# First weight piece and x in four pairs of 256 rows, first two tiles accumulated together, second piece's low part on VectorE

## The chip, the cores and the metric

The kernel runs on one core of one Trainium2 chip. The metric is the time of one execution on the device in microseconds (us); the time before is the median of 3 runs.

## The reference

Two layers of a streaming encoder trunk on x of 512 tokens by 1024 channels, float32. Each layer is

```
x <- LN(alpha * x + Mix(x))
x <- LN(alpha * x + MoE(x))
```

Mix multiplies x by one input projection (`h = x @ w_in + b_in`, 1024 to 1792 columns) and gives the columns to three groups: a gated causal depthwise convolution of 31 taps (256 channels, `a * sigmoid(g)`), a sliding-window attention of 8 query and 2 key heads with rotation of the first 16 dimensions, and a gated spatial mixing. Their 1024 outputs go through `w_out`. MoE is a router that picks 2 of 16 experts for each token, and a SwiGLU with 512 hidden channels in each expert.

## The kernel before

**Precision.** Each float32 matrix product is made from three products of a faster type: both operands are split into a high part (ScalarE's copy, which rounds) and a low part (the rest, by a subtraction on VectorE or GpSimd), and TensorE adds high x high, low x high and high x low (`product`, L392). So an operand takes three steps before TensorE can use it: transfer, high, low.

**Pieces.** The columns of `w_in` are reordered (gate half of the convolution first, then its value half, then q, k and v, the rest) and loaded in seven pieces of 256 columns and all 1024 rows (1 MB each, `load_piece`, L291); three further-on pieces come from `w_out`. Raw pieces go to two buffers `wraw` in turn, split pieces to three slots `wh`/`wl` in turn. In the traces `wraw` has the name `w_gate`, because it lies in that buffer, and x before its split has the name `w_up`. ScalarE makes a piece's high part (`piece`, L785), with `piece_high` counting them. GpSimd makes the low parts of pieces 1 to 8 of layer 0 (`piece_lows`, L1440), and VectorE that of piece 0 (L1324); `piece_low` counts them. SyncE issues all loads in order; piece q waits for `piece_low` >= q - 1.

**Tiles.** A piece gives two tiles of 128 output channels by 512 tokens (`channels(q, m)`, L403): 8 row blocks of 128 times three products, 24 in all, into one PSUM bank. Layer 0 begins with `channels(0, 0)`, `channels(1, 0)`, `channels(0, 1)`, `channels(1, 1)` (L434 to L437) into banks 0 to 3, each counted in `proj_done`. Later tiles go to banks 0 and 1 in turn and wait until the tile two before was read (`proj_act`, `proj_dve`). The sixth tile, `channels(2, 1)`, so waits for `gate_conv(1)`, which reads bank 3.

**The start.** SyncE issues piece 0, x in four parts of 256 rows (512 KB each), a table, piece 1 and further tables. ScalarE copies piece 0, then the four x parts, then piece 1. VectorE makes piece 0's low part and then the four of x, and TensorE's first tile waits for the x parts one by one.

**VectorE's queue in the projection of layer 0** is in a fixed order (L1329 on): `gate_conv(0)` (L1041; it waits for `proj_done` 2 and ScalarE's sigmoid, and is the first user of the tiles), the 31 taps of the first 128 channels (L1053 to L1057), `gate_conv(1)` before its seventeenth tap, then the taps of the other 128 channels with five rotations (`rope`, L1028) strewn in: L1032 multiplies the permuted tile (PSUM) by the sine, L1033 the tile by the cosine (both in SBUF), L1034 adds (both in SBUF). Then `mask_set`, for which the first scores on TensorE wait.

**ScalarE's queue** has the tiles' copies out of PSUM (L810, L818 and following) with the high parts of later pieces among them at fixed places: piece 5 behind the sixth tile's copy, piece 6 behind the eighth's, piece 7 behind the tenth's. GpSimd makes each low part when its high part is there.

## Time and profile before

| | us |
|---|---|
| median of the runs | 1137.98 (1137.33 to 1139.25) |
| profiled execution | 1142.18 |
| its span | 1140.4 |
| TensorE busy | 965.8 (85%) |
| VectorE busy | 807.7 (71%) |
| ScalarE busy | 648.9 (57%) |
| GpSimd busy | 521.6 (46%) |

The span is what the profile shows from the first to the last instruction; the execution's own time is 1.8 us more. The engines are named PE (TensorE's products), DVE (VectorE), ACT (ScalarE), POOL (GpSimd) and SP (SyncE, which issues the loads); a "q" behind a name is the engine's sequencer. L12 is line 12 of the kernel. A clock of 1.00 is TensorE's full clock, 2.4 GHz. Shares of the whole span mix stages with different limits, so the stages have to be read one by one.

### The profile page before, as it was taken

The numbers are of one execution on the slowest core, as the hardware profiler recorded it, in microseconds if no ns is written. First come the engines' busy times: TensorE is split into PE (matmuls) and PEld (weight loads), VectorE is DVE, ScalarE is ACT, GpSimd is POOL, SyncE is SP. The second block draws the span as 40 slices with busy tenths as digits, with TensorE's granted clock in tenths as the row PEclk, the third lists the DMA queues.
The fourth block names the chain that finished last, engine by engine and source line by source line (L and its number), as shares of the span: only waits on it lengthen the run. The fifth ranks groups of instructions, "written<-read, shape, count | busy, mean of one in ns | idle before, by whom it ended". The sixth has DMA issues, their size and how long they took to land. (4 is left out here: it accounts for less than half of the span.)

```text
span 1140.4 us, 15102 instructions
## 1 busy us (share of the span) xinstructions
PE 965.8 (85%) x4700; PEld 780.4 (68%) x4700; DVE 807.7 (71%) x964; ACT 648.9 (57%) x723; POOL 521.6 (46%) x297
## 2 busy tenths in 40 slices
PE   4998998289999999999269979982899999999950
PEld 3866775168888887878268757751688888888840
DVE  2996755567778787777467967555677787878737
ACT  4224712078878887877213347120788787878730
POOL 3435354035656556565205453440356565564621
PEclk9998998679999999999679989986799999999985
DMA  8521183079999999963713211930799999999625
GB/s 271 187 81 39 57 331 147 1 263 360 373 368 366 381 355 371 364 264 108 227 38 111 74 46 51 336 146 3 265 373 378 370 357 372 352 370 367 255 114 143
DMA packets 122511, 268.99 MB, mean 236 GB/s; under 512 B 10608, under 2 KB 26128, under 8 KB 121968
## 3 DMA queue, kind: packets, MB, share of 16 engines
q1 hardware_dynamic: 110192, 243.99, 59.0%
q0 software_dynamic: 12288, 24.60, 6.7%
q8 instruction: 17, 0.28, 0.1%
q14 instruction: 14, 0.11, 0.0%
HBM read 263.38 MB, written 24.64 MB: 253 GB/s over the span
## 5 line engine op out<-in xcount | busy, mean ns | idle before, releaser
L1500 POOL TENSOR_TENSOR wl<-w_down,wh 128x2048 fp32r<-128x2048 f32 x33 | 151.6, 4595 | 165.5 <-ACT wh L937 165.5
L1026 DVE TENSOR_TENSOR wl<-w_gate,wh 128x2048 fp32r<-128x2048 f32 x71 | 166.0, 2339 | 58.3 <-ACT wh L937 30.4
L1026 DVE TENSOR_TENSOR wl<-w_up,wh 128x2048 fp32r<-128x2048 f32 x66 | 151.2, 2293 | 29.5 <-ACT wh L937 29.1
L702 PE MATMUL bank<-wh,xTh 128*128 128x512 f32 x528 | 143.4, 394 | 4.5 <-ACT wh L937 4.5
L937 ACT ACTIVATE wh<-w_down 128x2048 fp32r<-128x2048 f32 x66 | 126.8, 1921 | 30.0 <-PE bank L702 30.0
L702 PE MATMUL bank<-wh,xTl 128*128 128x512 f32 x528 | 142.8, 393 | 0.0
L702 PE MATMUL bank<-wl,xTh 128*128 128x512 f32 x528 | 142.8, 393 | 0.0
L937 ACT ACTIVATE wh<-w_up 128x2048 fp32r<-128x2048 f32 x66 | 126.5, 1917 | 25.5 <-PE bank L720 24.9
L1444 POOL TENSOR_TENSOR wl<-w_gate,wh 128x2048 fp32r<-128x2048 f32 x17 | 78.0, 4593 | 135.5 <-ACT wh L794 135.2
L1026 DVE TENSOR_TENSOR xTl<-bank,xTh 128x512 fp32r<-128x512 f32 (+1 forms) x168 | 89.9, 574 | 62.5 <-ACT xTh L941 24.7
L396 PE MATMUL bank<-xTh,wh 128*128 128x512 f32 (+2 forms) x272 | 112.2, 412 | 24.9 <-DVE xTl L1026 21.1
L937 ACT ACTIVATE wh<-w_gate 128x2048 fp32r<-128x2048 f32 x66 | 126.5, 1916 | 7.7 <-PE bank L720 7.7
L702 PEld LDWEIGHTS bank<-wh,xTh 128*128 128x128 f32 x528 | 100.3, 190 | 26.2 <-issue 5.3
L702 PEld LDWEIGHTS bank<-wh,xTl 128*128 128x128 f32 x528 | 100.3, 190 | 21.1
L702 PEld LDWEIGHTS bank<-wl,xTh 128*128 128x128 f32 x528 | 100.3, 190 | 21.0
L396 PE MATMUL bank<-xTh,wl 128*128 128x512 f32 (+2 forms) x272 | 105.4, 387 | 0.0
L396 PE MATMUL bank<-xTl,wh 128*128 128x512 f32 (+2 forms) x272 | 105.1, 386 | 0.0
L1479 POOL DMA_INDIRECT moemem<-x_rows,gather_idx x35 | 81.6, 2330 | 30.6 <-POOL gather_idx L1476 30.6
L941 ACT ACTIVATE xTh<-bank 128x512 fp32r<-128x512 f32 x66 | 39.1, 593 | 92.4 <-PE bank L674 92.4
L396 PEld LDWEIGHTS bank<-xTh,wh 128*128 128x128 f32 (+1 forms) x272 | 53.8, 198 | 41.3 <-issue 17.9
L1026 DVE TENSOR_TENSOR wl<-w_down,wh 128x2048 fp32r<-128x2048 f32 x33 | 75.7, 2293 | 7.9 <-ACT wh L937 7.9
L1057 DVE SCALAR_TENSOR_TENSOR bank<-w_down,col,bank 128x512 f32<-128x512 f32 x116 | 77.7, 747 | 1.7 <-DVE w_down L1041 0.5
(206 smaller groups left out, 1726.5 us busy)
## 6 DMA issues: line engine op xcount, KB each, us to landing
w_up<-in_exp_w_up SPq DMA_DIRECT2D x32, 2048.0 KB, 13.3
w_down<-in_exp_w_down SPq DMA_DIRECT2D x32, 2048.0 KB
w_gate<-in_exp_w_gate SPq DMA_DIRECT2D x32, 2048.0 KB, 12.6
w_gate<-in_w_in SPq DMA_DIRECT2D x14, 1024.0 KB, 5.5
w_gate<-in_w_out SPq DMA_DIRECT2D x8, 1024.0 KB, 5.0
x_rows<-xtok POOLq DMA_DIRECT2D x8, 512.0 KB, 3.0
w_gate<-in_rows_mix SPq DMA_DIRECT2D x2, 1536.0 KB, 6.3
w_up<-in_x_t SPq DMA_DIRECT2D x4, 512.0 KB, 7.5
```

Of the source, the lines that this page charges most:

```text
L396: mm = pe.matmul(out, xs[i], ws[k], start=(first and n == 0), stop=(last and n == 2))
L702: mm = pe.matmul(bank[piece][:, :], xgT[m][:, 4 * (i % 2) + k, :], w[q][:, k, :], start=(i % 2 == 0 and n == 0 and k == 0), stop=(i % 2 == ...
L937: act.activation(wh[s][:, :], slot[r][p][:, cols], ACT.Copy).then_inc(half_high, 1)
L941: act.activation(xgT[0][:, 4 * i:4 * i + 4, :], bank[2 + i][:, :].rearrange("p (k t) -> p k t", k=4), ACT.Copy).then_inc(xgT_high, 1)
L1026: return dve.tensor_tensor(out, src, high.bitcast(F32), ALU.subtract)
L1057: y = dve.scalar_tensor_tensor(o, x, wk, o, ALU.mult, ALU.add)
L1444: pool.tensor_tensor(wl[n % SLOTS][:, :], wraw[n % 2], wh[n % SLOTS][:, :].bitcast(F32), ALU.subtract)\
L1479: pool.indirect_dma_start(xg, None, x1d[l], bass.IndirectOffsetOnAxis(ap=gather_idx[:, :], axis=0), bounds_check=T - 1, oob_is_err=False). ...
L1500: pool.tensor_tensor(wl[s][:, :], slot[r][p][:, cols], wh[s][:, :].bitcast(F32), ALU.subtract)\
```

## The change

Layer 0 only. SyncE loads the first piece in four parts of 256 rows, each followed by the x part of the same rows (`head`), and ScalarE and VectorE split them in this order. TensorE runs along the four pairs and accumulates both tiles of the first piece, in banks 0 and 2, 12 products for each pair; then come the two tiles of the second piece, in banks 1 and 3. `proj_done` then counts bank 0, bank 2, bank 1, bank 3, so `gate_conv(0)` waits for a count of 3. VectorE, not GpSimd, makes the second piece's low part. GpSimd begins with piece 2.

```diff
--- before.py
+++ after.py
@@ -197,6 +197,8 @@
         wexp_in = [[sem(f"{n}_in{r}") for n in ("gate", "up", "down")] for r in range(2)]
         dve_chain, pool_chain = sem("dve_chain"), sem("pool_chain")
         xT_high, xT_low = sem("xT_high"), sem("xT_low")
+        head_in = [sem(f"head_in{i}") for i in range(4)]
+        head_high, head_low = sem("head_high"), sem("head_low")
         piece_high, piece_low, last_low = sem("piece_high"), sem("piece_low"), sem("last_low")
         proj_done = sem("proj_done")
         proj_act, proj_dve = sem("proj_act"), sem("proj_dve")
@@ -261,6 +263,10 @@
 
             return bank[4 + 2 * (j % 2) + i] if q % 2 else bank[4 * i + j]
 
+        def head(x, i):
+
+            return x[:, 512 * i:512 * i + 512].rearrange("p (k n) -> p k n", k=2)
+
         def halves(i):
 
             return i // 2, slice(2048 * (i % 2), 2048 * (i % 2) + 2048), i % SLOTS
@@ -318,12 +324,13 @@
 
             for l in range(DEPTH):
                 if l == 0:
-                    load_piece(l, 0)
-                    sp.dma_start(xraw[:, 0:2, :], a["x_t"][0:256, :].rearrange("(k p) t -> p k t", p=P))\
-                      .then_inc(xT_in[0], 16)
-                    for i in range(1, 4):
-                        sp.dma_start(xraw[:, 2 * i:2 * i + 2, :], a["x_t"][256 * i:256 * i + 256, :]
-                                     .rearrange("(k p) t -> p k t", p=P)).then_inc(xT_in[i], 16)
+                    for i in range(4):
+                        rows = slice(256 * i, 256 * i + 256)
+                        sp.dma_start(head(wraw[0], i), a["w_in"][l, rows, 0:PIECE].rearrange("(k p) n -> p k n", p=P))\
+                          .then_inc(head_in[i], 16)
+                        sp.dma_start(xraw[:, 2 * i:2 * i + 2, :], a["x_t"][rows, :].rearrange("(k p) t -> p k t", p=P))\
+                          .then_inc(xT_in[i], 16)
+                    sp.sem_inc(wraw_in[0], 16)
                     sp.dma_start(col[:, :], a["cols"][l]).then_inc(col_in, 16)
                     load_piece(l, 1)
                     sp.dma_start(cst[:, :], a["const"]).then_inc(const_in, 16)
@@ -413,8 +420,6 @@
                     n = (PIECES * l + q) % SLOTS
                     w = [x[:, :].rearrange("p (k n) -> p k n", k=KD) for x in (wh[n], wl[n])]
                     for k in range(KD):
-                        if l == 0 and t == 0 and k % 2 == 0:
-                            pe.wait_ge(xT_low, k // 2 + 1)
                         mm = product(bank[t if t < 4 else t % 2][:, c], [w[i][:, k, P * m:P * m + P] for i in range(2)],
                                      [xparts[i][:, k, c] for i in range(2)], k == 0, k == KD - 1)
                     if part != 0:
@@ -431,10 +436,19 @@
                     pe.matmul(bank[4 + n % 2][:, :], perm, src, start=True, stop=True).then_inc(rot_done, 1)
 
                 if l == 0:
-                    channels(0, 0)
-                    channels(1, 0)
-                    channels(0, 1)
-                    channels(1, 1)
+                    w = [x[:, :].rearrange("p (k n) -> p k n", k=KD) for x in (wh[0], wl[0])]
+                    for i in range(4):
+                        pe.wait_ge(head_low, i + 1)
+                        pe.wait_ge(xT_low, i + 1)
+                        for m in range(2):
+                            for k in (2 * i, 2 * i + 1):
+                                mm = product(bank[2 * m][:, :], [w[h][:, k, P * m:P * m + P] for h in range(2)],
+                                             [xparts[h][:, k, :] for h in range(2)], k == 0, k == KD - 1)
+                            if i == 3:
+                                mm.then_inc(proj_done, 1)
+                    for t in (1, 3):
+                        task[0] = t
+                        channels(1, t // 2)
                 else:
                     q = 2 * l - 1
                     turn(q, 0)
@@ -795,11 +809,14 @@
 
             def project(l):
                 if l == 0:
-                    piece(l, 0)
                     for i in range(4):
+                        act.wait_ge(head_in[i], 16)
+                        act.activation(head(wh[0], i), head(wraw[0], i), ACT.Copy).then_inc(head_high, 1)
                         act.wait_ge(xT_in[i], 16)
                         act.activation(xparts[0][:, 2 * i:2 * i + 2, :], xraw[:, 2 * i:2 * i + 2, :], ACT.Copy)\
                            .then_inc(xT_high, 1)
+                    act.wait_ge(head_high, 4)
+                    act.sem_inc(piece_high, 1)
                     piece(l, 1)
                 act.wait_ge(col_in, 16 * (l + 1))
                 for m in range(2):
@@ -1036,7 +1053,7 @@
 
             def gate_conv(l, m):
 
-                dve.wait_ge(proj_done, PROJ * l + 2 * m + 2)
+                dve.wait_ge(proj_done, PROJ * l + (3 if l == 0 and m == 0 else 2 * m + 2))
                 dve.wait_ge(sig_set, 2 * l + m + 1)
                 link(dve.scalar_tensor_tensor(glu[:, m, TAPS - 1:], bank[2 * m + 1][:, :],
                                               col[:, C_BIN + 2 + m:C_BIN + 3 + m], u[:, m, :], ALU.add, ALU.mult))
@@ -1320,12 +1337,15 @@
             dve.sem_inc(he_set, 1)
             link(dve.memset(eps, EPS))
             link(dve.memset(mhalf, -0.5))
-            dve.wait_ge(piece_high, 1)
-            low(wl[0][:, :], wraw[0], wh[0][:, :]).then_inc(piece_low, 1)
             for i in range(4):
+                dve.wait_ge(head_high, i + 1)
+                low(head(wl[0], i), head(wraw[0], i), head(wh[0], i)).then_inc(head_low, 1)
                 dve.wait_ge(xT_high, i + 1)
                 low(xparts[1][:, 2 * i:2 * i + 2, :], xraw[:, 2 * i:2 * i + 2, :], xparts[0][:, 2 * i:2 * i + 2, :])\
                     .then_inc(xT_low, 1)
+            dve.wait_ge(head_low, 4)
+            dve.sem_inc(piece_low, 1)
+            piece_lows(0, 1)
             for l in range(DEPTH):
                 dve.wait_ge(col_in, 16 * (l + 1))
                 link(dve.memset(glu[:, :, 0:TAPS - 1], 0.0))
@@ -1512,8 +1532,8 @@
             for l in range(DEPTH):
                 if l == 0:
 
-                    pool.wait_ge(piece_low, 1)
-                for q in range(1 if l == 0 else 3, 7):
+                    pool.wait_ge(piece_low, 2)
+                for q in range(2 if l == 0 else 3, 7):
                     piece_lows(l, q)
 
                 piece_lows(l, 7)
```

## Rows read from the trace of the kernel before

**Rows 1.** Stretches: from:to and length, busy us of each engine, PE clock, DMA share, GB/s.
```profile
39.90:52.00 12.10, 12.10 (x53) 9.70 (x52) 11.72 (x20) 3.89 (x4) 6.60 (x2) 1.00 0.56 175
52.00:90.00 38.00, 33.84 (x163) 26.43 (x161) 36.36 (x51) 10.76 (x12) 13.79 (x3) 0.96 0.24 83
232.00:580.00 348.00, 314.67 (x1447) 256.68 (x1446) 263.06 (x216) 257.72 (x231) 182.69 (x109) 0.95 0.87 314
```

**Rows 2.** Waits of TensorE, 0 to 140 us: who for whom, total, times, longest.
```profile
PE bank L396 <- DVE xTl L1026: 11.9, 1, 11.9
PE bank L536 <- DVEq L1347: 2.8, 1, 2.8
PE bank L396 <- POOL wl L1444: 2.5, 1, 2.5
```

**Rows 3.** Waits of all engines, 80 to 110 us.
```profile
POOL w_down L1522 <- DVEq L1353: 6.8, 1, 6.8
```

**Rows 4.** Instructions in time order, 0 to 22 us: start, duration, engine, line, operation.
```profile
6.28 1.91 ACT L794 ACTIVATE wh<-w_gate 128x2048 fp32r<-128x2048 f32 x1 [4.18 <-DMA w_gate<-in_w_in]
...
8.30 2.29 DVE L1026 TENSOR_TENSOR wl<-w_gate,wh 128x2048 fp32r<-128x2048 f32 x1 [6.98 <-ACT wh L794]
...
10.51 4.62 DVE L1026 TENSOR_TENSOR xTl<-w_up,xTh 128x1024 fp32r<-128x1024 f32 x4
...
11.75 1.06 ACT L801 ACTIVATE xTh<-w_up 128x1024 fp32r<-128x1024 f32 x1 [0.33 <-DMA w_up<-in_x_t]
...
11.88 0.77 PE L396 MATMUL bank<-xTh,wh 128*128 128x512 f32 x1 [11.88 <-DVE xTl L1026]
...
14.88 1.92 ACT L794 ACTIVATE wh<-w_gate 128x2048 fp32r<-128x2048 f32 x1 [2.08 <-DMA w_gate<-in_w_in]
...
18.71 0.39 PE L396 MATMUL bank<-xTl,wh 128*128 128x512 f32 x1
19.19 1.28 ACT L810 ACT_TABLE_LOAD   x1 [2.39 <-PE bank L396]
...
21.91 1.91 ACT L794 ACTIVATE wh<-w_gate 128x2048 fp32r<-128x2048 f32 x1 [0.74 <-DMA w_gate<-in_w_in]
```

**Rows 5.** Stretches of one us each: DMA share and GB/s come last.
```profile
2.00:3.00 1.00, 0.00 (x0) 0.00 (x0) 0.00 (x0) 0.11 (x1) 0.00 (x0) 1.00 0.74 175
3.00:4.00 1.00, 0.00 (x0) 0.00 (x0) 0.00 (x0) 0.00 (x0) 0.00 (x0) 1.00 1.02 358
4.00:5.00 1.00, 0.00 (x0) 0.00 (x0) 0.00 (x0) 0.00 (x0) 0.00 (x0) 1.00 1.08 379
```

**Rows 6.** VectorE in time order, 29 to 70 us.
```profile
29.01 0.75 DVE L1041 SCALAR_TENSOR_TENSOR w_down<-bank,col,w_down 128x512 f32<-128x512 f32 x1 [13.80 <-PE bank L396]
...
40.59 0.74 DVE L1041 SCALAR_TENSOR_TENSOR w_down<-bank,col,w_down 128x512 f32<-128x512 f32 x1
...
55.83 2.60 DVE L1033 TENSOR_TENSOR w_gate<-w_gate,w_down 128x512 f32<-128x512 f32 x1
...
63.39 0.69 DVE L1034 TENSOR_TENSOR w_gate<-w_gate,w_down 128x512 f32<-128x512 f32 x1
...
68.90 2.22 DVE L1033 TENSOR_TENSOR w_gate<-w_gate,w_down 128x512 f32<-128x512 f32 x1
```

**Rows 7.** ScalarE and GpSimd in time order, 50 to 70 us.
```profile
50.72 0.69 ACT L818 ACTIVATE w_gate<-bank,col 128x512 f32<-128x512 f32 x1 [4.75 <-PE bank L396]
...
53.28 4.60 POOL L1444 TENSOR_TENSOR wl<-w_gate,wh 128x2048 fp32r<-128x2048 f32 x1 [6.77 <-ACT wh L794]
65.98 4.59 POOL L1444 TENSOR_TENSOR wl<-w_gate,wh 128x2048 fp32r<-128x2048 f32 x1 [8.09 <-ACT wh L794]
```

**Rows 8.** TensorE behind a wait: two stretches with clock, and the second wait.
```profile
19.50:24.50 5.00, 2.94 (x8) 2.31 (x9) 0.00 (x0) 3.57 (x3) 2.61 (x2) 0.74 0.69 198
152.00:155.00 3.00, 2.71 (x12) 2.21 (x13) 0.24 (x1) 0.00 (x0) 3.00 (x2) 1.00 1.05 414
...
152.29 0.50 PE L396 MATMUL bank<-wh,xTh 128*128 128x512 f32 x1 [1.42 <-DVE xTl L1026]
```

## The prediction

> **What bounds the kernel now.** I read four views in this order: the busy times of stretches, the waits, the first 22 us in order of time, and then VectorE's and GpSimd's own timelines up to 90 us.
>
> The stretches [rows 1] show two kinds of stage. In the expert stage TensorE is busy 315 of 348 us: nothing of the change is there. In the projection of layer 0 TensorE and VectorE are both full: from 39.9 to 52 us VectorE is busy 11.72 of 12.10 us, from 52 to 90 us 36.36 of 38. Which of the two sets the end is told by the waits [rows 2]: TensorE waits 11.9 us for the first split of x, 2.5 us for the second weight piece (GpSimd's low part), and then 2.8 us at the first scores, for a VectorE semaphore (mask_set). GpSimd also waits 6.8 us for VectorE there [rows 3]. VectorE has no such wait for TensorE after its first real work at 29.01 us [rows 6]. So until the scores the chain is: start of VectorE's gate_conv(0) at 29.01, then its queue of taps and rotations without a gap. TensorE is ahead of it and loses its lead by waiting at the end. Whatever moves VectorE's start, or shortens its queue, moves the rest.
>
> **Step 1, the first product.** Now TensorE starts at 11.88 [rows 4], behind a 1 MB piece copied whole (1.91 us), its low (2.29) and the first x low. With the change it needs 256 KB of weights and 512 KB of x. Bytes delivered by the end of each us [rows 5]: 0.19 MB at 3, 0.55 at 4, 0.93 at 5 (with 0.01 before 2). The old first piece, 1.05 MB, is reached at 5.33, and its copy starts at 6.28: 0.95 us later. The new first pair is 0.79 MB, reached at 4.63; I take 1.0 us for the landing: ScalarE's copy of x starts at 5.63 (its copy of the 256 KB is done by then: 4.2 to 4.8, a quarter of 1.91 plus overhead), takes 1.06 (the row of the x part), 0.11 passes to VectorE (6.28 + 1.91 to 8.30), and from the start of an x low to the first product is 1.37 (10.51 to 11.88). First product T = 5.63 + 1.06 + 0.11 + 1.37 = 8.2, so 3.7 earlier. Bounds: 7.2 if the landing costs nothing, 11.88 if the pair arrives no sooner than piece and x do now.
>
> **Step 2, the start of VectorE's queue.** gate_conv(0) reads bank 1, which is now the third tile, not the second. A tile is 24 products. The first tile's 24 starts spread over 6.83 us (11.88 to 18.71), because the clock rises only on the way; afterwards a product takes 0.228 us (53 products in 12.10 us, [rows 1]). The reader of a tile starts 0.48 after its last product starts (18.71 to 19.19). So gate_conv(0) starts at S = T + 6.83 + 48 x 0.228 + 0.48 = T + 18.3 = 26.4, if TensorE never stops on the way. Against 29.01 that is **2.6 us earlier**. The extra tile in front (5.5 us) eats more than the earlier start alone gives; the rest comes from two removed losses: the 2.5 us wait for piece 1, and the slow clock behind it [rows 8].
>
> Does TensorE stop? Pairs: 768 KB come every 2 us at 380 GB/s, ScalarE needs about 0.6 + 1.06 for a pair, VectorE 0.6 + 1.16 (4.62 over four, [rows 4]), TensorE 12 x 0.228 = 2.7 or more: TensorE is the slowest, and no pair is late. The last pair's x copy starts as now at 11.75, since the bytes ahead of it are the same, and VectorE ends its low near 14.1, while TensorE needs it at T + 36 products, near 18. Piece 1: same bytes ahead, so its copy starts at 14.88 as now and ends at 16.8; VectorE's low (2.29, where GpSimd takes 4.6, [rows 7]) ends at 19.2. TensorE asks for it at T + 6.83 + 25 x 0.228 = 20.7. Cover: 1.4 us; each us beyond that costs a us. The low delays nothing on VectorE, which is idle until 26.4.
>
> SyncE issues three more transfers (about 0.5 us each) ahead of piece 1, but all are issued by about 6 us, long before their bytes flow. Piece 2's issue waits for piece_low 1, which moves from 10.6 (8.30 + 2.29) to 14.1. Its copy starts at 21.91 now [rows 4], 7.8 us after that, and 1 MB at 380 GB/s is 2.8 us: nothing. ScalarE makes this copy behind the sigmoid of bank 0; bank 0 ends at T + 6.83 + 18 x 0.228 + 0.48, about 19.6 against 19.19, so this slips by at most 0.4; its low is ready near 29 (1.9 + 4.6 behind), and TensorE asks for it one tile behind S, near 31.6. Piece 3's copy waits for proj_done 3 as before, the end of the third tile, which comes earlier now.
>
> **Step 3, the stalls inside VectorE's queue.** Rope multiplies x by cosine, both in SBUF (L1033). This takes 0.69 us, but 2.60 at 55.83 and 2.22 at 68.90 [rows 6], and both times GpSimd's piece low runs (53.28 to 57.88, 65.98 to 70.57, [rows 7]); the multiply ends 0.55 us behind it. Taps and the PSUM sources keep their length beside GpSimd. So an SBUF-only operation of VectorE stands still until GpSimd's is over.
>
> The Trainium skill ("SBUF — State Buffer", section "SBUF: two separate sides") says that the pair of ports shared by both is an exclusive lock for the whole instruction, also for a VectorE operation with two SBUF inputs. By that rule, the trace agrees (2.60 against 0.69), and the sum is the same by row and by rule.
>
> What matters is where the lows fall after the change. TensorE's fifth tile ends near T + 6.83 + 96 x 0.228 + 0.3, about 37.1, and the sixth must wait until gate_conv(1) has read bank 3: now that ends 11.58 + 0.74 behind the queue's start (29.01 to 40.59, [rows 6]), so it starts at S + 12.4 = 38.8. TensorE idles 1.7 us, and from here both engines are locked relative to S. The sixth tile is copied 5.7 later, S + 18.1, and the piece low starts 2.56 behind this copy (50.72 to 53.28, [rows 7]): S + 20.7 to S + 25.3. The first L1033 is at S + 26.8: free, 1.91 us saved. The next low is 12.70 later, S + 33.4 to 38.0; the third rope's L1033 comes at 39.9 - 1.9 = S + 38.0: just free, 1.53 saved. The low after that (12.7 later again, S + 46.1 to 50.7) meets the fifth rope's multiply at about S + 50.4 (a rope every 6.2 us: the second's last operation at 63.39, so its multiply at 62.7, and the third's at 68.90); I count nothing. Sum of step 3: **3.4 us**. Bounds: 0 (all stay) and below nothing, see the rivals.
>
> **Carry.** At the scores TensorE, ScalarE and GpSimd wait for VectorE [rows 2, 3], all orders behind are relative to that, and the expert stage takes its time from TensorE. So 2.6 + 3.4 = 6.0 us reach the end. The profiled execution took 1142.18 (span 1140.4 and 1.8 around it), which gives 1136.2; the median of the runs is 4.2 lower, 1137.98, and gives **1132.0**.
>
> **Rivals.**
> (a) The clock falls in the new 1.7 us wait before tile six. For: behind the 2.5 us wait the granted clock is 0.74 of full over 5 us [rows 8]. Against: a wait of 1.42 at 152.29 left it at 1.00 (2.4 GHz). Price: TensorE 1.4 later (6.83 against 24 x 0.228), so the second low covers the third rope again: 1.4 of the 3.4 is lost, time 1133.4.
> (b) Only the head start comes, the collisions stay in number because the lags behind a tile differ from those I carried over: 2.6 gained, 1135.4. For: the second rests on a margin near 0.
> (c) The pairs don't land one by one but close together. For: eight transfers are outstanding at once. Against: rows 5 with the copies at 6.28, 11.75 and 14.88 show landing in order of issue. With T = 11.88 again, S = 30.1, 1.1 later than now, and step 3, which hangs on S alone, still gives 3.4: 1135.7. The Trainium skill ("DMA: Bandwidth & Descriptors", section "Anatomy of one DMA — SWDGE (gpsimd) path") gives a fixed part of about 2.0 us for each transfer, measured on another issue path than this one; if it were paid one after another, four x parts could not have been copied by 12.8 us as they are, so the trace speaks against that reading.
> (d) Slower: GpSimd's lows land on the rope before. The second rope's two SBUF operations end near S + 33.2 (63.39 + 0.69 - 29.01 - 1.91, [rows 6]), and the low begins at S + 33.4. If it began before S + 32.5, that is 0.9 sooner relative to VectorE than I find, it would hold the second operation until 37.1 + 0.55: 4.4 us. The fourth rope's multiply, due at S + 44.2 and now at 48.6, would then meet the next low until 50.7 + 0.55, 2.6 more. 7.0 lost against 6.0 gained: 1139.0. Up to that point it costs nothing; from there it decides.
>
> **Chances.** Forecast 0.52, (a) 0.13, (b) 0.18, (c) 0.10, (d) 0.07. Under 0.2% (2.3 us) from 1137.98 a measurement here can't tell a change; that is 1135.7. Faster: forecast, (a), most of (b), half of (c), together 0.80. Same: the rest of (b) and (c), 0.13. Slower: 0.07. The range reaches down to 1129.8 (T at 7.2, another us in the ropes behind) and up to 1136.5, which holds (b) and (c) and leaves out (d).
>
> **What would show it.** First product near 8.2, no wait of TensorE between pairs or at the third tile, L1041 first at 26.4; the first and third L1033 at 0.69; a wait of TensorE of about 1.7 before tile six, its clock at full behind it; scores 6 us earlier, and the same 6 us at the first expert. Wrong would be: a first product after 10, a wait for piece 1, any L1033 or L1034 over 2 us, or a gain at the scores that is gone at the experts.

## The result, and the profile after

| | median | runs | |
|---|---|---|---|
| before, same chip | 1138.62 us | 1137.33 to 1140.45 | 4 |
| changed | 1146.88 us | 1143.21 to 1148.92 | 4 |

The ratio is 1.0068, 95% interval 1.0038 to 1.0097: the change made the kernel 0.7% slower, where 1132.0 us was forecast. Repeated on another chip it gave 1144.59 against 1138.36, ratio 1.0059 (1.0032 to 1.0085). The profiled execution took 1143.21 us, the lowest of its runs, while that of before, 1142.18, was above all the runs shown with it. The two traces alone thus differ by 1 us, the medians by 6 to 8; where it can be done I compare several executions.

First the head of the kernel. This is the timeline of the changed kernel up to 39 us (start, duration, engine, line, operation; in brackets the idle time before and what ended it), against [rows 4]:
```profile
3.81 0.63 ACT L814 ACTIVATE wh<-w_gate 128x512 fp32r<-128x512 f32 x1 [1.71 <-DMA w_gate<-in_w_in]
...
5.17 1.06 ACT L816 ACTIVATE xTh<-w_up 128x1024 fp32r<-128x1024 f32 x1 [0.73 <-DMA w_up<-in_x_t]
...
6.26 1.23 DVE L1043 TENSOR_TENSOR xTl<-w_up,xTh 128x1024 fp32r<-128x1024 f32 x1 [1.02 <-ACT xTh L816]
...
7.63 0.77 PE L403 MATMUL bank<-xTh,wh 128*128 128x512 f32 x1 [7.63 <-DVE xTl L1043]
...
12.98 1.06 ACT L816 ACTIVATE xTh<-w_up 128x1024 fp32r<-128x1024 f32 x1 [0.53 <-DMA w_up<-in_x_t]
...
16.12 1.92 ACT L808 ACTIVATE wh<-w_gate 128x2048 fp32r<-128x2048 f32 x1 [2.08 <-DMA w_gate<-in_w_in]
...
18.07 2.29 DVE L1043 TENSOR_TENSOR wl<-w_gate,wh 128x2048 fp32r<-128x2048 f32 x1 [2.77 <-ACT wh L808]
...
26.27 0.75 DVE L1058 SCALAR_TENSOR_TENSOR w_down<-bank,col,w_down 128x512 f32<-128x512 f32 x1 [5.84 <-PE bank L403]
...
38.71 0.50 PE L403 MATMUL bank<-xTh,wh 128*128 128x512 f32 x1 [1.66 <-DVEq L1060]
```
The first product comes at 7.63 (was 11.88), VectorE's queue starts at 26.27 (was 29.01), and TensorE's wait ahead of the sixth tile is 1.66: 8.2, 26.4 and 1.7 had been forecast. That part did what it should.

The waits of TensorE from 0 to 140 us (who for whom, total, times, longest) answer to [rows 2]:
```profile
PE bank L550 <- DVEq L1367: 9.0, 1, 9.0
...
PE bank L403 <- DVE xTl L1043: 7.6, 1, 7.6
...
PE bank L436 <- DVEq L1052: 2.0, 1, 2.0
...
PE bank L403 <- DVEq L1060: 1.7, 1, 1.7
```
The wait for piece 1 (2.5) is gone and the one for x is 4.3 shorter, but the wait at the scores is 9.0 instead of 2.8, and ahead of it, at 65.83, there is a new one of 2.0 for L1052, the end of the second rope. The scores start at 88.21, against 85.66 before: of 2.7 us of head start nothing is left, and 2.6 are lost. The stretches show the same as [rows 1] do, TensorE's busy time in the second of them falling from 33.84 to 26.86 us while VectorE stays full:
```profile
39.90:52.00 12.10, 12.10 (x52) 9.26 (x51) 11.97 (x16) 3.78 (x4) 7.32 (x2) 1.00 0.62 211
52.00:90.00 38.00, 26.86 (x125) 20.74 (x124) 36.50 (x48) 7.64 (x7) 9.19 (x2) 0.90 0.24 83
```

Where VectorE loses it is on its own timeline (compare [rows 6]) beside GpSimd's (compare [rows 7]). A low of GpSimd is here the subtraction that makes the low part of one piece:
```profile
48.95 2.80 DVE L1358 CAST utri<-w_down 128x128 bf16<-128x128 f32 x1
...
55.66 0.69 DVE L1050 TENSOR_TENSOR w_gate<-w_gate,w_down 128x512 f32<-128x512 f32 x1
...
60.59 4.32 DVE L1050 TENSOR_TENSOR w_gate<-w_gate,w_down 128x512 f32<-128x512 f32 x1
...
76.69 3.46 DVE L1050 TENSOR_TENSOR w_gate<-w_gate,w_down 128x512 f32<-128x512 f32 x1
```
```profile
47.07 4.59 POOL L1464 TENSOR_TENSOR wl<-w_gate,wh 128x2048 fp32r<-128x2048 f32 x1 [4.43 <-ACT wh L808]
...
59.76 4.59 POOL L1464 TENSOR_TENSOR wl<-w_gate,wh 128x2048 fp32r<-128x2048 f32 x1 [8.11 <-ACT wh L808]
...
75.01 4.59 POOL L1464 TENSOR_TENSOR wl<-w_gate,wh 128x2048 fp32r<-128x2048 f32 x1 [10.65 <-ACT wh L808]
```
L1050 is the multiply of a rope (L1033 before); shown are the first, second and fourth, and the third and fifth took 0.69. The first one is now free, as forecast. But a cast of a 128 x 128 constant in front of it took 2.80 us: GpSimd's low ran from 47.07 to 51.66, and the cast ended 0.09 us behind it. Before, the cast took 0.23 us. Two rows of before that the prediction did not use, the cast and the fifth rope:
```profile
51.69 0.23 DVE L1338 CAST utri<-w_down 128x128 bf16<-128x128 f32 x1
...
82.91 0.92 DVE L1033 TENSOR_TENSOR w_gate<-w_gate,w_down 128x512 f32<-128x512 f32 x1
```
VectorE is 2.57 us late from there. The second low of GpSimd starts at 59.76, the second rope's multiply comes at 60.59 and ends only at 64.91 (4.32 us). TensorE waits 2.0 us for the end of this rope, and the third low comes 15.25 us behind the second, where the prediction had 12.7. It begins at 75.01, the fourth rope's multiply at 76.69: 3.46. Excess over the undisturbed lengths: 2.57 + 3.63 + 2.77 = 8.97 us. Before it was 1.91 + 1.53 + 0.23 = 3.67 for the first, third and fifth rope. The difference, 5.3 us, is the whole of what lies between VectorE's start and the scores (88.21 - 26.27 = 61.94, before 85.66 - 29.01 = 56.65).

### The profile page after: what moved, and what is told of

It reads as the page before. It is cut to its first block and busy times, and to the rows that moved or that the text cites. A ratio compares the mean times of both kernels' runs of the same rounds, so it can differ in the third digit from the quotient of the medians.

```text
span 1141.4 us, 15117 instructions
## 1 busy us (share of the span) xinstructions
PE 965.4 (85%) x4700; PEld 778.2 (68%) x4700; DVE 814.7 (71%) x968; ACT 650.0 (57%) x726; POOL 520.0 (46%) x296
## 5 line engine op out<-in xcount | busy, mean ns | idle before, releaser
L1043 DVE TENSOR_TENSOR wl<-w_gate,wh 128x2048 fp32r<-128x2048 f32 (+1 forms) x75 | 168.8, 2252 | 55.7 <-ACT wh L954 27.6
L1464 POOL TENSOR_TENSOR wl<-w_gate,wh 128x2048 fp32r<-128x2048 f32 x16 | 73.5, 4603 | 136.1 <-ACT wh L808 135.7
```

The lines of the kernel that those rows point to most:

```text
L1043: return dve.tensor_tensor(out, src, high.bitcast(F32), ALU.subtract)
L1464: pool.tensor_tensor(wl[n % SLOTS][:, :], wraw[n % 2], wh[n % SLOTS][:, :].bitcast(F32), ALU.subtract)\
```

## The experiments

Milestones of all the profiled executions, in us: S, the start of VectorE's queue (its first read of bank 1); the scores; TensorE's 1.42 us wait late in layer 0's mixing; the first tile of layer 1; the same 1.42 us wait in layer 1; the first expert of layer 1; TensorE's last product.

| kernel | S | S to scores | scores | late mixing | layer 1 | late mixing 1 | expert, layer 1 | expert to end |
|---|---|---|---|---|---|---|---|---|
| before | 29.01 | 56.65 | 85.66 | 152.29 | 579.66 | 723.14 | 801.26 | 297.2 |
| before_again | 27.21 | 56.65 | 83.86 | 150.26 | 576.55 | 717.41 | 795.40 | 297.2 |
| before_pad7 | 27.43 | 56.64 | 84.07 | 148.88 | 574.74 | 718.47 | 796.82 | 298.7 |
| changed | 26.27 | 61.94 | 88.21 | 152.74 | 578.46 | 722.15 | 800.36 | 299.1 |
| after_again | 26.92 | 61.95 | 88.87 | 153.62 | 579.76 | 723.38 | 801.31 | 299.0 |
| pool_low1 | 29.51 | 63.52 | 93.03 | 159.44 | 586.13 | 729.88 | 807.97 | 297.5 |
| pairs_old_order | 26.84 | 56.63 | 83.47 | 149.89 | 577.29 | 720.62 | 798.79 | 298.9 |
| cast_early | 26.83 | 53.18 | 80.01 | 144.84 | 571.35 | 715.01 | 793.12 | 299.0 |
| cast_taps | 26.83 | 53.50 | 80.33 | 145.75 | 572.10 | 715.82 | 794.09 | 298.8 |
| cast_pool | 26.30 | 53.15 | 79.45 | 145.69 | 571.99 | 715.79 | 794.30 | 297.1 |
| dve_low1 | 25.27 | 56.65 | 81.92 | 147.30 | 573.80 | 717.53 | 795.95 | 297.4 |
| dve_low1_taps | 25.68 | 56.69 | 82.37 | 145.55 | 571.43 | 722.71 | 800.50 | 297.4 |
| dve_low1_taps0 | 24.86 | 56.79 | 81.65 | 143.25 | 568.81 | 712.79 | 790.74 | 297.1 |

And the times. The kernels from one entry in the column of before to the next ran on one chip and share its runs of the kernel before; the ratio is to those, with its 95% interval.

| kernel | median us | runs | before, same chip | ratio |
|---|---|---|---|---|
| after_again | 1144.59 | 5 | 1138.36 | 1.0059 (1.0032 to 1.0085) |
| cast_early | 1135.43 | 10 | | 0.9971 (0.9962 to 0.9981) |
| pool_low1 | 1148.44 | 4 | | 1.0081 (1.0056 to 1.0107) |
| cast_taps | 1135.28 | 8 | | 0.9968 (0.9954 to 0.9983) |
| dve_low1 | 1135.95 | 10 | 1137.68 | 0.9976 (0.9960 to 0.9991) |
| pairs_old_order | 1140.58 | 9 | | 1.0036 (1.0023 to 1.0049) |
| dve_low1_taps | 1139.68 | 10 | | 1.0020 (1.0003 to 1.0036) |
| before_again | 1136.38 | 1 | | |
| cast_pool | 1134.27 | 8 | 1138.29 | 0.9967 (0.9951 to 0.9983) |
| before_pad7 | 1140.13 | 12 | | 1.0014 (1.0003 to 1.0025) |
| dve_low1_taps0 | 1133.78 | 6 | | 0.9959 (0.9944 to 0.9974) |

**after_again**: the changed kernel, nothing edited.

> The changed kernel, unaltered, for a second profile and a second set of times. Theory A (stalls of VectorE's queue behind GpSimd's lows of pieces 5, 6 and 7: the cast of utri 2.80, the multiply of the second rope 4.32, that of the fourth 3.46): the three stalls are there again at the same offsets from the start of the queue (22.7, 34.3 and 50.4 us behind it), together near 9.0 us, and the first scores start near 88.2 us. Rival B (the time is lost behind the scores, in the attention, the expert stages or layer 1, and the first projection has nothing to do with it): the scores near 88.2 again, but the second profile's span is several us over the first's 1141.4 with the first 88 us alike.

Measured 1144.59 us. The three long operations are there again, and from S to the scores it takes 61.95 us against 61.94: the loss is of the program, not of one execution.

**cast_early**: the changed kernel with the cast moved in front of VectorE's first read of a bank, where VectorE is idle.

```diff
                 link(dve.memset(glu[:, :, 0:TAPS - 1], 0.0))
+                if l == 0:
+                    dve.wait_ge(mixc_in, 16)
+                    dve.tensor_copy(utri[:, :], mixc[:, M_UTRI:M_UTRI + P]).then_inc(ones_set, 1)
                 gate_conv(l, 0)
...
-                if l == 0:
-                    dve.wait_ge(mixc_in, 16)
-                    dve.tensor_copy(utri[:, :], mixc[:, M_UTRI:M_UTRI + P]).then_inc(ones_set, 1)
```

> The changed kernel with the cast of utri put before gate_conv(0), where VectorE is idle. Theory A: the cast takes 0.2 us there; the queue then reaches the ropes 2.8 us earlier, ahead of GpSimd's low of piece 6, so the second rope's multiply takes 0.69; the third's may meet the end of that low (under 1.2), the fourth's is free, the fifth's may meet the low of piece 7. Stalls together 2 us in place of 9.0, first scores near 81 us in place of 88.2, and the time 6 to 8 us under the changed kernel's. Rival B: scores earlier, but the time stays within 2 us of the changed kernel's.

Measured 1135.43 us, 9.2 below the changed kernel in the same runs, from the place of one instruction of 0.23 us. VectorE's timeline, the cast and the multiplies of the second and fourth rope (the third took 0.81, the fifth 0.94):
```profile
21.08 0.23 DVE L1354 CAST utri<-w_down 128x128 bf16<-128x128 f32 x1
...
58.43 0.69 DVE L1050 TENSOR_TENSOR w_gate<-w_gate,w_down 128x512 f32<-128x512 f32 x1
...
71.02 0.69 DVE L1050 TENSOR_TENSOR w_gate<-w_gate,w_down 128x512 f32<-128x512 f32 x1
```
and GpSimd's, the two lows that had caught the ropes:
```profile
60.33 4.59 POOL L1464 TENSOR_TENSOR wl<-w_gate,wh 128x2048 fp32r<-128x2048 f32 x1 [8.09 <-ACT wh L808]
...
73.02 4.62 POOL L1464 TENSOR_TENSOR wl<-w_gate,wh 128x2048 fp32r<-128x2048 f32 x1 [8.10 <-ACT wh L808]
```
With the cast gone the second rope starts 1.90 ahead of the low at 60.33, and the fourth 2.00 ahead of the next. The scores start at 80.01, S + 53.18, where after_again has S + 61.95: 8.8 sooner. The rule of the stalls and the prediction's arithmetic of them (3.4 us off the 56.65 of before) are confirmed: the scores come 3.47 sooner behind S, 3.30 from shorter multiplies and the rest from the cast's own place in the queue. What the prediction lacked was the cast.

**cast_taps**: cast_early, and one or two taps moved between the ropes, so that no rope touches a low.

```diff
-                for n, hi in enumerate((8, 14, 20, 26)):
+                for n, hi in enumerate((8, 15, 21, 27)):
...
-                    taps(1, hi - (4 if n == 0 else 6), hi)
+                    taps(1, (4, 8, 15, 21)[n], hi)
...
-                taps(1, 26, TAPS)
+                taps(1, 27, TAPS)
```

> cast_early, and one tap more between the second and the third rope (taps 8 to 15, 15 to 21, 21 to 27 in place of 8 to 14, 14 to 20, 20 to 26), so that the third and fifth ropes' multiplies come 0.7 us later, behind GpSimd's lows of pieces 6 and 7. Theory A: no operation of VectorE in the projection is stretched by over 0.3 us, first scores near 79.5 us, time 1 to 2 us under cast_early's. Rival B: the time is cast_early's.

Measured 1135.28 us, the same as cast_early (1135.43), where 1 to 2 less were expected. All five multiplies are at 0.69, but the extra tap stands ahead of the scores (S + 53.50 against 53.18). A rest of stall of 0.37 us was not worth the 0.7 us of one more tap ahead of the scores.

**pool_low1**: the changed kernel with the second piece's low back on GpSimd.

```diff
-            piece_lows(0, 1)
             for l in range(DEPTH):
                 dve.wait_ge(col_in, 16 * (l + 1))
...
-                    pool.wait_ge(piece_low, 2)
-                for q in range(2 if l == 0 else 3, 7):
+                    pool.wait_ge(piece_low, 1)
+                for q in range(1 if l == 0 else 3, 7):
```

> The changed kernel with the low part of piece 1 made by GpSimd, as before the change; pairs and order of tiles stay. GpSimd takes 4.6 us in place of 2.3, so the third tile starts near 22.7 in place of 20.3 and the clock may fall in that wait of about 2: VectorE's queue starts at 28.5 to 30 in place of 26.3. Theory A: everything behind hangs on that start, so the same three stalls follow at the same offsets, scores near 90.5 to 92, time 2 to 4 us over the changed kernel. Rival B: no change or any.

Measured 1148.44 us, 3.9 over the changed kernel on the same chip. TensorE waits 2.99 us for the piece, and S is 29.51:
```profile
23.67 0.50 PE L403 MATMUL bank<-xTh,wh 128*128 128x512 f32 x1 [2.99 <-POOL wl L1463]
```
The same three operations stand still, the last one for longer:
```profile
52.18 2.79 DVE L1357 CAST utri<-w_down 128x128 bf16<-128x128 f32 x1
...
63.81 4.31 DVE L1050 TENSOR_TENSOR w_gate<-w_gate,w_down 128x512 f32<-128x512 f32 x1
...
79.90 5.07 DVE L1050 TENSOR_TENSOR w_gate<-w_gate,w_down 128x512 f32<-128x512 f32 x1
```
So the low on VectorE is what gives the head start (2.6 of it), and the stalls don't come from it: they come with the order of tiles.

**dve_low1**: the kernel before, and only the second piece's low moved to VectorE.

```diff
+            piece_lows(0, 1)
             for l in range(DEPTH):
                 dve.wait_ge(col_in, 16 * (l + 1))
...
-                    pool.wait_ge(piece_low, 1)
-                for q in range(1 if l == 0 else 3, 7):
+                    pool.wait_ge(piece_low, 2)
+                for q in range(2 if l == 0 else 3, 7):
```

> The kernel before with one part of the change alone: the low part of piece 1 by VectorE (2.3 us) in place of GpSimd (4.6). Theory A: the second tile starts at 19.2 in place of 21.56, without a wait, so the clock stays up and VectorE's queue starts near 25.2, earlier than with the whole change (26.3). TensorE then doesn't wait before its sixth tile, so GpSimd's lows of pieces 5, 6 and 7 stand later against the queue: the cast stays at 0.23, the first rope's multiply meets a low (about 3.2), the third's too (about 2.2), the fifth's perhaps. First scores near 82.5, time 3 to 4 us under the kernel before. Rival C (the earlier start of the queue is what does the harm, however it comes): the cast or the second rope's multiply over 2 us, and no gain.

Measured 1135.95 us, ratio 0.9976. VectorE's queue starts at 25.27, sooner than in any kernel of the change, and both stalls of before stay:
```profile
25.27 0.75 DVE L1041 SCALAR_TENSOR_TENSOR w_down<-bank,col,w_down 128x512 f32<-128x512 f32 x1 [6.21 <-PE bank L396]
...
52.09 2.60 DVE L1033 TENSOR_TENSOR w_gate<-w_gate,w_down 128x512 f32<-128x512 f32 x1
...
65.16 2.23 DVE L1033 TENSOR_TENSOR w_gate<-w_gate,w_down 128x512 f32<-128x512 f32 x1
```
The whole gain of the start is in this one edit; the four pairs and the order of tiles bring VectorE nothing over it (26.3 to 26.9). The gain in time is 1.7 us where 3 to 4 were expected: the S of before to compare with is 27.2 or 27.4, as before_again and before_pad7 show, not 29.01.

**pairs_old_order**: the changed kernel, but the pairs feed bank 0 alone, and the tiles then follow as before.

```diff
-                        for m in range(2):
-                            for k in (2 * i, 2 * i + 1):
+                        for k in (2 * i, 2 * i + 1):
...
-                    for t in (1, 3):
-                        task[0] = t
-                        channels(1, t // 2)
+                    task[0] = 1
+                    channels(1, 0)
+                    channels(0, 1)
+                    channels(1, 1)
```

> The changed kernel with the old order of tiles: only the first half of the first piece is multiplied along the pairs, then channels(1,0), (0,1), (1,1). The first tile ends near 17, TensorE waits about 3.5 for piece 1 and its clock falls, VectorE's queue starts near 27.9. Theory A: TensorE does not wait before its sixth tile, so the lows stand as in the kernel before: cast 0.23, first and third rope's multiply stretched to about 2.8 and 2.2, second and fourth 0.69; scores near 84.9, time 0.5 to 1.5 us under the kernel before. Rival C: as the queue starts 1.1 us earlier than before, cast or second rope over 2 us and a loss.

Measured 1140.58 us, slower than before where somewhat faster was expected. TensorE has nothing to do between the first tile and piece 1:
```profile
19.50 0.80 PE L403 MATMUL bank<-xTh,wh 128*128 128x512 f32 x1 [3.39 <-DVE wl L1043]
```
The cast is free again while the multiplies are as long as before:
```profile
49.52 0.23 DVE L1358 CAST utri<-w_down 128x128 bf16<-128x128 f32 x1
...
53.66 2.58 DVE L1050 TENSOR_TENSOR w_gate<-w_gate,w_down 128x512 f32<-128x512 f32 x1
...
66.72 2.21 DVE L1050 TENSOR_TENSOR w_gate<-w_gate,w_down 128x512 f32<-128x512 f32 x1
```
From S to the scores it takes 56.63 us, as in the kernel before. So, with the same queue of VectorE, it is the order of tiles that decides which operations are caught. TensorE has no wait before its sixth tile here, and the first of the three lows starts at S + 24.3, as before; in the changed kernel it is S + 20.8. The scores come at 83.47, 0.4 sooner than in before_again, and yet the kernel's median is 2.9 us higher. The table shows where 1.7 of it is: expert to end 298.9 against 297.2, a loss that is in the changed kernel as well and does not lie in layer 0. The rest, 1.2 us, stays open. This set off the third group of runs.

**dve_low1_taps**: dve_low1, the cast moved as in cast_early, and the taps between the ropes as (7, 11, 17, 23, 29), in both layers.

```diff
-                taps(1, 0, 4)
-                for n, hi in enumerate((8, 14, 20, 26)):
+                taps(1, 0, 7)
+                for n, hi in enumerate((11, 17, 23, 29)):
```

> dve_low1 with the cast where VectorE is idle and three taps more ahead of the first rope (taps 7, 11, 17, 23, 29 in place of 4, 8, 14, 20, 26), which puts every rope between two of GpSimd's lows. Theory A: all five multiplies at 0.7, mask_set at a time near 82 (the ropes end 2 us later in the queue, the stalls of 4 us are gone), scores near 82 but the last tap 3 to 4 us earlier than in dve_low1; time 1 to 3 us under dve_low1's, the lowest of all. Rival B: no better than dve_low1.

Measured 1139.68 us: a miss. Layer 0 gained (late mixing at 145.55 against 147.30 in dve_low1), though its third rope's multiply still took 2.22 us where 0.7 was expected. But the same cuts in layer 1 brought its ropes under GpSimd's lows:
```profile
630.72 5.02 DVE L1033 TENSOR_TENSOR w_gate<-w_gate,w_down 128x512 f32<-128x512 f32 x1
...
647.53 3.48 DVE L1033 TENSOR_TENSOR w_gate<-w_gate,w_down 128x512 f32<-128x512 f32 x1
```
From the first tile of layer 1 to its late mixing it takes 151.3 us against 143.7.

**before_again**: the kernel before, nothing edited, for one more profile.

> The kernel before, unaltered, for a second profile: the first took 4 us more than the median of its timed runs. Theory A: the first 85.66 us are the same (cast 0.23, first and third rope's multiply 2.6 and 2.2), and the 4 us lie elsewhere. Rival D: the first profile had stretched operations in the first projection that a usual execution has not, so the loss of the change at the scores, 2.55 us by the two profiles, is understated.

It took 1136.38 us. The first 86 us are not those of the first trace. The stretch of [rows 8] and the products behind the wait for piece 1:
```profile
19.50:24.50 5.00, 3.16 (x15) 2.58 (x15) 0.00 (x0) 3.89 (x3) 2.61 (x2) 1.00 0.69 215
```
```profile
21.37 0.50 PE L396 MATMUL bank<-xTh,wh 128*128 128x512 f32 x1 [1.84 <-POOL wl L1444]
...
27.21 0.75 DVE L1041 SCALAR_TENSOR_TENSOR w_down<-bank,col,w_down 128x512 f32<-128x512 f32 x1 [12.21 <-PE bank L396]
```
TensorE waited 1.84 us instead of 2.5, and its granted clock stayed at 1.00 (2.4 GHz) where it had been 0.74. S is 27.21, 1.8 sooner, and from S on everything is equal up to the scores (56.65 both times). So 29.01 was the bad side of a chance; before_pad7, for TensorE the same kernel up to here, has 27.43. The three traces differ first within the first tile. Its products start 0.43 us apart and later 0.23; the step comes after 7 intervals in before, 10 in before_again and 13 in before_pad7. The later the first tile ends, the shorter is the wait for piece 1: 2.46, 1.84 and 1.34 us. Behind the wait of 2.46 the products are 0.43 apart again for 8 intervals, behind the other two they are not.

**cast_pool**: cast_early, but the cast on GpSimd, which changes VectorE's program by one instruction.

```diff
-                    dve.wait_ge(mixc_in, 16)
-                    dve.tensor_copy(utri[:, :], mixc[:, M_UTRI:M_UTRI + P]).then_inc(ones_set, 1)
...
+                    pool.wait_ge(mixc_in, 16)
+                    pool.tensor_copy(utri[:, :], mixc[:, M_UTRI:M_UTRI + P]).then_inc(ones_set, 1)
                     pool.wait_ge(piece_low, 2)
```

> The changed kernel with the cast of utri made by GpSimd, before its first low, while both are idle. VectorE has one instruction less than in cast_early. Theory A: ropes as in cast_early (0.69 to 0.94), first scores near 80.0. Theory E (place of the code): in the profiles so far a pair of experts of layer 1 takes 36.43 us in the kernels with 747, 748 and 750 counted VectorE instructions and 36.63 in those with 751, with VectorE 0.6 us longer at the branch back of the loop over pairs; so with 750 the stage of layer 1, first gathered transposition to TensorE's last, is 297.3 in place of 299.0, and the time 1.5 to 2 us under cast_early's 1135.4. Against E: 299.0 again and the time of cast_early.

**before_pad7**: the kernel before with seven small memsets at the beginning of VectorE's program, where it is idle.

```diff
             link(dve.memset(mhalf, -0.5))
+            for _ in range(7):
+                link(dve.memset(idle[:, :], 0.0))
```

> The kernel before with seven tiny memsets more on VectorE while it waits for the first piece; they take well under 1 us of its 7 us of idle time and write an unused cell. Theory E: the code behind them moves by at least as much as in the changed kernel, VectorE's gap at the branch of the pair loop in layer 1 grows by 0.6 us, the expert stage of layer 1 takes 299.0 in place of 297.2, time 1.5 to 2 us over the kernel before. Against E: 297.2 and no change of the time. Either way the profile shows once more where gate_conv(0) starts in the kernel before: 29.0 as in the first profile or 27.2 as in the second.

These two belong together. before_pad7 is slower than before by 1.8 us (1140.13, ratio 1.0014), with 298.7 from the expert to the end; cast_pool has 297.1, as the kernel before, and took 1134.27 us. That its time lies below cast_early's is not shown by the times alone: against the kernel before on their own chips the ratios are 0.9967 and 0.9971, well within each other's intervals. Take VectorE's instructions as the profile's page counts them, each turn of a loop for itself (the numbers in the expectation are lower by 217 throughout): before has 964, the dve_low1 kernels 965, pool_low1 and cast_pool 967, and all of these have 297.1 to 297.5. The changed kernel, after_again, pairs_old_order, cast_early and cast_taps have 968, before_pad7 has 971, and these have 298.7 to 299.1. What is lost is seen in VectorE's waits from 812 to 1080 us, the experts of layer 1 (who for whom, total, times, longest). Before:
```profile
DVE xTl L1026 <- issue: 9.7, 7, 1.4
```
Changed:
```profile
DVE xTl L1043 <- issue: 11.7, 7, 2.0
```
before_pad7:
```profile
DVE xTl L1026 <- issue: 11.6, 7, 2.0
```
cast_pool:
```profile
DVE xTl L1043 <- issue: 9.5, 7, 1.4
```
There is a gap of VectorE in which it waits for nothing that the profile shows once in each turn of the loop over pairs of experts, where the loop branches back. In before all seven are 1.4 us; in the changed kernel the first is 2.0 and the six others 1.6 (together the 11.7 above). The first one in the changed kernel, and TensorE's wait that follows from it:
```profile
836.81 0.41 DVE L1304 TENSOR_TENSOR moemem<-bank,moemem 128x256 f32<-128x256 f32 x1
...
839.18 0.69 DVE L1043 TENSOR_TENSOR xTl<-bank,xTh 128x512 fp32r<-128x512 f32 x1 [1.96 <-issue]
...
840.25 0.96 PE L734 MATMUL bank<-wh,xTl 128*128 128x512 f32 x3 [0.20 <-DVE xTl L1043]
```
From one such gap to the next it takes 36.63 us instead of 36.43. The 0.6 us expected for every gap holds for the first one only; the others grow by 0.24. The loss goes with the number of VectorE instructions, and before_pad7 shows that instructions without any use are enough for it. How instructions ahead of a loop make its branch longer, and whether their place or their number counts, no run shows. Layer 0's loop is not touched: from its first expert to layer 1 it takes 348.3 to 349.5 us in all kernels, on either side of the count.

**dve_low1_taps0**: dve_low1, the cast moved, and the taps between the ropes changed in layer 0 alone.

```diff
-                taps(1, 0, 4)
-                for n, hi in enumerate((8, 14, 20, 26)):
+                cuts = (7, 11, 19, 25, 31) if l == 0 else (4, 8, 14, 20, 26)
+                taps(1, 0, cuts[0])
+                for n, hi in enumerate(cuts[1:]):
```

> dve_low1 with the cast where VectorE is idle and with the ropes of layer 0 alone moved (taps 7, 11, 19, 25, 31; layer 1 as before, where the earlier move of both layers stretched two multiplies to 5.0 and 3.5). Queue start near 25.5. Theory A: no multiply of layer 0 over 1.1 us, first scores near 82.3 (the ropes now end the queue), layer 1 as in dve_low1; time 2 to 3 us under dve_low1's 1136. Rival B: dve_low1's time, since the scores come no earlier.

Measured 1133.78 us (1131.57 to 1134.68), ratio 0.9959 (0.9944 to 0.9974): the lowest median of the study, below both the kernel before and the changed one (1.0059 and 1.0068 of before). Its interval overlaps those of cast_pool, cast_taps and cast_early, so that it is faster than these is not shown. It keeps the kernel before's loads and its order of tiles. The first and third rope in VectorE's timeline:
```profile
24.86 0.75 DVE L1041 SCALAR_TENSOR_TENSOR w_down<-bank,col,w_down 128x512 f32<-128x512 f32 x1 [5.50 <-PE bank L396]
...
53.54 0.81 DVE L1033 TENSOR_TENSOR w_gate<-w_gate,w_down 128x512 f32<-128x512 f32 x1
...
66.13 0.91 DVE L1033 TENSOR_TENSOR w_gate<-w_gate,w_down 128x512 f32<-128x512 f32 x1
```
The scores come no sooner than in dve_low1, since all 31 taps now stand ahead of them, but what had followed the scores is shorter: late mixing at 143.25 against 147.30.

## Why the prediction was wrong, step by step

**Step 1, right.** First product at 7.63, forecast 8.2. VectorE's first low of x started at 6.26, where 6.80 had been worked out (5.63 + 1.06 + 0.11); ScalarE's copy of x started at 5.17, so by the bytes of [rows 5] (0.79 MB at 4.63) the landing costs 0.5 and not the 1.0 us assumed.

**Step 2, right in its place, with two flaws.** S = 26.27 for 26.4, no wait between pairs, none at the third tile, 1.66 before the sixth. But the bytes being the same did not keep the times: the fourth x copy came at 12.98 instead of 11.75, and piece 1's at 16.12 instead of 14.88, with its low ready at 20.36. The second x copy came 3.57 us behind the first, where 2 us for a pair had been reckoned; the other two followed in 2.13 and 2.11. Of the cover of 1.4 us next to nothing was left: in after_again TensorE waited 0.33 for it, in cast_early 0.74. The second flaw is that 29.01 was read as the kernel's start, when it was one execution's: it holds a fall of the clock that [rows 8] showed and I counted as a loss the change removes. In before_again and before_pad7 it did not happen. The head start over such executions is 0.3 to 1.2 us (26.27 and 26.92 against 27.21 and 27.43), not 2.6. An execution profiled 4.2 us above the median of the runs was the hint. The 6.83 us of the first tile are one execution's as well: 7.47 in before_again, 7.97 in before_pad7, 6.90 in the changed kernel. That the clock rises on the way is seen in the distance of the products, 0.43 and then 0.23 us; the profile's granted clock is 1.00 throughout the stretch.

**Step 3, failed, and this decides the sign.** "So an SBUF-only operation of VectorE stands still until GpSimd's is over": true. The low was forecast at S + 20.7 and began at S + 20.8. I then looked at the ropes alone. The cast from L1338 of before (L1358 after) is SBUF-only too and stood in the queue between the taps, at 51.69 = S + 22.7, in the middle of the forecast low. It was in the trace at 0.23 us and looked free, because before the change no low ran beside it: the next began 1.4 us behind its end. The low was moved off the first rope onto the cast; VectorE then came 2.57 late to the second low, whose margin for the second rope had been worked out as 0.9. From there rival (d) took its course, at its places (second and fourth rope) and almost at its price (the second rope's multiply 3.63, the fourth's 2.77, against 4.4 and 2.6). The 2.6 was worked out wrongly: from 48.6 to 50.7 + 0.55 less the 0.69 that the multiply takes anyway is 2.0, so (d) as described costs 6.4 and gives 1138.4, not 1139.0. I had given it 0.07 because it wanted VectorE 0.9 us late and I had looked for a reason in the lags of GpSimd, not in VectorE's queue. -3.4 was forecast for this step, +5.3 came. The Trainium skill ("SBUF — State Buffer", section "Who interferes with whom") names copy and cast among the operations that can take the pair of ports shared with GpSimd, when their operands meet the conditions of a two-port mode; I had drawn on its rule for two inputs alone. The trace agrees for this cast (2.80 against 0.23 us).

**Carry, right in part.** Of what is lost at the scores about two thirds go through: from before_again to after_again it is 5.0 us there, 3.4 at the late mixing, 3.2 at layer 1. To this come 1.8 us in the experts of layer 1, which go with the number of VectorE's instructions; the prediction had put the expert stages at nothing. Together 5 us; between medians on one chip it was 6.2, in the first measurement 8.3. The 1 to 3 us between stay open. before_again itself shows how far single executions differ: its layer 1 takes 140.9 us up to the late mixing, where all others but dve_low1_taps have 143.3 to 144.0.

**Rivals.** (a) is out: the granted clock is 1.00 in the stretch from 39.90, behind the 1.66 us wait. (b) is out: it had the collisions of before, and the first and third rope are free. (c) is out: the four x copies start at 5.17, 8.74, 10.87 and 12.98, one pair after the other, and TensorE had no wait between them. (d) is what happened.

## What to carry to other kernels

Before moving work of one engine in time against another's, write down every operation of the first that can stand still beside the other's, the small ones too, each with its distance to the edge of the other's spans: an instruction of 0.23 us cost 9.2. Take the start times of before from more than one execution, above all behind a wait after which the clock was low. And when only the count of instructions in front of a long loop changes, compare the loop's own period before and after: here it grew from 36.43 to 36.63 us.

## What the runs showed of the hardware

- A 128 x 128 cast of VectorE within SBUF stood still while GpSimd worked through a 128 x 2048 subtraction, and ended 0.09 us behind it (2.80 us for 0.23); so did multiplies with both inputs in SBUF, which ended 0.56 us behind it (4.32 and 3.46 us for 0.69). Taps with a PSUM operand kept 0.75 us beside it.
- VectorE's gaps at a loop's branch were 1.4 us in the kernels whose VectorE runs 964 to 967 instructions. With 968 or 971 the first gap was 2.0 and the six others 1.6 us, and only in the second of two loops.
- The same program with a wait of 1.84 us kept a granted clock of 1.00, and with one of 2.5 us had 0.74 behind it, 1.8 us of difference in the start of the next engine. The length of the wait does not settle it: behind 3.39 us in pairs_old_order the same stretch had 0.68, but behind 2.99 us in pool_low1 the clock was 1.00 (23.67 to 28.67).
- With three more transfers and the same bytes ahead of a piece of 1 MB its copy started between 15.21 and 17.00 us in the seven traces, and between 14.66 and 14.88 in the six with the old loads.
